# Two orders on TensorE in layer AB: values' second half ahead of q and k in the first loop; the time step's projection behind the first product with v

## The chip, the cores and the metric

The kernel is one program on one core of a Trainium2 chip. Time is the device time of one execution in microseconds (us); the profile's times are counted from the start of its span. The engines are TensorE (PE: matmuls and transposes, its weight loads listed apart as PEld), VectorE (DVE), ScalarE (ACT), GpSimd (POOL), and SyncE (SP), whose queue issues nearly all DMAs.

## What is computed

One inference step of a two-layer streaming encoder, for a prompt of 2048 tokens and a sample of 32 tokens that share all weights. The first layer (AB in the kernel) normalizes x and projects it with one input matrix. Group A is a gated linear attention with 4 heads of 64 keys and 128 values:

```
q_a, k_a, v_a, glow, z_a, q_b, k_b, v_b, z_b = split(rms_norm(x) @ w_in)
g = log_sigmoid(glow @ w_gate_up + b_gate) / 16              # decay per token and key
per chunk:  b = cumsum(g);  qe = q * exp(b)
   o = tril(qe @ (k * exp(-b)).T) @ v + qe @ S
   S = exp(b_last) * S + (k * exp(b_last - b)).T @ v
o_a = rms_norm(o) * silu(z_a)
```

Group B is attention over a window of 128 rows with 8 query heads, 2 key heads, learned sinks and a position bias; its output is gated by silu(z_b). Both go through one output projection and are added to x. The second layer (C) is a Mamba-2 scan with a causal convolution; its step `dt` is a 32-column projection of the normalized output of layer AB, made by softplus, together with the running sum of dt*A over the tokens.

Outputs are y for prompt and sample, and the new states and caches.

## The kernel before

Rows of x are cut into 17 tiles: tile 0 is the sample (32 rows), tiles 1 to 16 are 128 rows each of the prompt. The program runs in phases with a barrier between them: `setup`, `layer_gla` (group A of the first layer, to about 545 us), `layer_swa` (group B, the output projection, the norm of the result and the step of layer C, to about 1355 us), `layer_c` and `project_c`. The change touches the PE programs of `layer_gla` and `layer_swa` alone.

Nothing plans the order of work. Each engine has its own program, written out by hand, and runs it strictly in order; semaphores join them. `tiles(start, step, end, eng)` calls `start` for tile 0, `step(x, n, m)` for each tile x with its two successors n and m, and `end` for the last one. `since(eng, sem, x, back, n)` waits until `sem` has been raised by the tile `back` ahead of x. Almost every product is made three times (high part by high part, high by low, low by high), so a projection with KT = 8 slices of 128 rows has 24 matmuls.

**layer_gla.** In `step(x, n, m)` PE projects tile n, finishes the attention of tile x and turns (transposes) tile m. The order is: `queries_keys(n)` (512 columns into bank B_QK), `attention(x)` (key by query products, L732, and the turned decayed keys, L737), `values(n)`, `gate_low(n)` (L751), `outputs(x)` (L774, L775, L779), `turn_qk(n)`, `gate_up(n)`, `turn_x(m)`, `gate(n)` (z, 512 columns into B_ZA), `turn_oa(x)` (L792). `values(n)` projects the second half of the values with the low-rank gate (272 columns, bank B_VG, L708), then the first half (256 columns, L744) and group B's k and v (256 columns, L708), both into B_V0. All projections but L744 are made by the helper `project`, so they share L708 and are told apart by their columns.

The psum has eight banks and some serve twice. B_ZA and B_QK are one bank: q and k of tile n may be written once DVE has made z's gate of tile x (`za_made`, L622). B_H, into which x is turned, is B_V0 and B_VG: both may be written again once DVE has taken the low part of the turned tile (`h_low`). On SP, `load_x` of the next tile stands behind the two stores of the gated output of the tile before (`store_oa`).

In `start`, tile 0 is projected while the weights still arrive: each slice k of the first projection waits for its weights (`w_low`, L565), the later projections find them made.

**layer_swa.** In `step(x, n, m)` PE's order is: `scores(x)`, `queries(n)`, `turn_weights(x, 0)` (L1415), `turn_x1(before)` (L1462), `gate(n)`, `steps_in(before)` (L1472, the projection for the time step), `turn_weights(x, 1)`, `weighted(x, 0)` (L1425, L1426: product of the softmax weights of heads 0 to 3 with v), `time_step(before)` (L1480, turns of dt and its running sum), `output_start(x, 0)` (12 matmuls of 512 columns, L1434), `weighted(x, 1)`, `output_start(x, 1)`, `turn_ob(x)`, `turn_q(n)`, `turn_k(n)`, `output_end(x)`. `before` is the tile ahead of x; the first step has none.

What feeds these: `steps_in(before)` needs the turned x1 of `before` in SBUF (`h2_half`, DVE L1250). `weighted(x, half)` needs the turned weights of that half copied to SBUF, one part by ACT (`pt0_copied`, L1039) and one by DVE (`pt1_copied`, L1208). ACT's order there is `weights_turned(x, 0)`, `time_step(before)` (L1066 to L1069: abs, exp, ln; needs `steps_in`), `window_gate(n)` (a table load L1084, tanh L1087, a table load L1088), `weights_turned(x, 1)`. DVE's order is `weights_turned(x, 0)`, `window_in(n)`, `turned_x1(before)`, `time_step(before)` (four small instructions, the last a scan, `dtac_made`), `weights_turned(x, 1)`, `weighted(x, 0)` (L1216), `time_step_tok(before)` (L1269, `dtok_made`), `window_gate(n)`, `weighted(x, 1)`.

The two halves of the output projection have a bank each, B_OUT[0] and B_OUT[1]. The turned x1 uses both, and the time step's projection and turns use the second (B_DT and B_DTT). Therefore the first half waited for both, turned x1 taken and token form copied:

```python
if n == 0:
    pe.wait_ge(s["oa_in"], 32 * x.t + 32)
    since(pe, s["dtok_made"], x, 1)
    since(pe, s["h2_half"], x, 1, 2)
```

Of the kernel before, what the change touches and what calls it, by code (L numbers as in the profile page):

```python
# [45 lines left out]
A_V1, A_KV = VA + 256, QB  # L46
A_VG = 256 + RANK
# [9 lines left out]
def names(nc, phase, text):  # L57

    return {n: nc.alloc_semaphore(f"{phase}_{n}") for n in text.split()}
# [227 lines left out]
def since(eng, sem, x, back, n=1):  # L287

    if not x.fixed or x.t >= back:
        eng.wait_ge(sem, n * (x.t - back + 1))  # L290


def layer_gla(nc, a, o, c, d, w, psum):

    with ExitStack() as ctx:
        def sb(name, shape, dtype=F32):
# [27 lines left out]
        s = names(nc, "gla", """w_high w_low x_in s0_in hT_out0 hT_out1 kv_out0 kv_out1 oa_out s_out  # L324
            act_x act_g act_o dve_x dve_g dve_o init0
            ssq_x var_x rs_x rstd_x xn_made h_full h_high h_low
            qk_full qk_copied vg_full v0_full vg_copied v0_copied glt_full glow_copied qkt_full
            gup_full g_abs g_ln b_scal eb_made q_made s_scaled kd_full kd_copied att_full att_copied
            za_full za_tanh za_made o_full o_sq o_var o_ln oa_made sup_full s_new oat_full oat_high oat_low""")
        block = ctx.enter_context(nc.Block())  # L330
        xp = a["x_prompt"][0].rearrange("(t r) m -> t r m", r=P)
        B_O, B_OAT, B_QK, B_V0, B_VG, B_G, B_ATT, B_QKT = psum
# [366 lines left out]
        def _(pe):  # L699
            M, T = nc.tensor.matmul, nc.tensor.transpose  # L700

            def project(out, x, col, n, full):

                for k in range(KT):
                    if x.sample:
                        pe.wait_ge(s["w_low"], k + 1)
                    for p, (h, wt) in enumerate(((hh, wh), (hh, wl), (hl, wh))):
                        ins = M(out, h[x.buf][:, k, 0:x.R], wt[:, k, col:col + n],  # L708
                                start=(k == 0 and p == 0), stop=(k == KT - 1 and p == 2))
                ins.then_inc(full, 1)  # L710

            def turn_x(x):
                pe.wait_ge(s["xn_made"], x.t + 1)
                since(pe, s["vg_copied"], x, 1)
                since(pe, s["v0_copied"], x, 1)
                for k in range(KT):
                    ins = T(B_H[k // 4][:, (k % 4) * P:(k % 4) * P + x.R], xn[0:x.R, k * P:(k + 1) * P], c["ident"][0:x.R, 0:x.R])
                    if k % 4 == 3:
                        ins.then_inc(s["h_full"], 1)

            def queries_keys(x):
                pe.wait_ge(s["h_low"], 2 * x.t + 2)
                since(pe, s["za_made"], x, 1)
                project(B_QK[0:x.R, :], x, 0, 512, s["qk_full"])

            def attention(x):
# [10 lines left out]
                    ins = T(B_KD[0:R, j * P:(j + 1) * P], ekd[:, j, 0:R], c["ident"][:, :])  # L737
                ins.then_inc(s["kd_full"], 1)

            def values(x):  # L740
                project(B_VG[0:x.R, 0:A_VG], x, A_V1, A_VG, s["vg_full"])
                for k in range(KT):
                    for p, (h, wt) in enumerate(((hh, wh), (hh, wl), (hl, wh))):
                        M(B_V0[0:x.R, 0:256], h[x.buf][:, k, 0:x.R], wt[:, k, VA:VA + 256],  # L744
                          start=(k == 0 and p == 0), stop=(k == KT - 1 and p == 2))
                project(B_V0[0:x.R, 256:512], x, A_KV, 256, s["v0_full"])

            def gate_low(x):
                pe.wait_ge(s["vg_copied"], x.t + 1)
                since(pe, s["b_scal"], x, 1)  # L750
                T(B_G[0:RANK, 0:x.R], vg[x.buf][0:x.R, 512 + 256:512 + A_VG], c["ident"][0:x.R, 0:x.R]).then_inc(s["glt_full"], 1)  # L751
# [31 lines left out]
            def gate(x):  # L783
                pe.wait_ge(s["qk_copied"], x.t + 1)
                project(B_ZA[0:x.R, :], x, ZA, 512, s["za_full"])
# [9 lines left out]
            def start(x, n):  # L795
                pe.wait_ge(s["init0"], 3)
                turn_x(x)
                queries_keys(x)
                values(x)
                gate_low(x)  # L800
                turn_qk(x)
                gate_up(x)
                turn_x(n)
                gate(x)

            def step(x, n, m):
                queries_keys(n)
                attention(x)
                values(n)
                gate_low(n)  # L810
                outputs(x)
                turn_qk(n)
                gate_up(n)
                if m is not None:
                    turn_x(m)
                gate(n)
                turn_oa(x)

            def end(x):
                attention(x)  # L820
                outputs(x)
                turn_oa(x)

            tiles(start, step, end, pe)
    return s


def layer_swa(nc, a, o, c, d, w, psum):

    with ExitStack() as ctx:  # L830
        def sb(name, shape, dtype=F32):
# [29 lines left out]
        s = names(nc, "swa", """w_in0 w_in1 w_high w_low kcache_in h_in kv_in oa_in x1_in fin_out x1_out hT_out dt_out  # L861
            act_q act_p act_n act_dt dve_q dve_k dve_m dve_d dve_n dve_dt
            init0 kcache_full kcache_kept pool_step kv_shifted bias_set
            qb_full qb_sq q_summed kv_sq v_copied qb_var qb_ln qn_made kn_made qtr_full qT_made ktr_full kz_made
            zb_full zb_tanh zb_made sc_full sc_added mx_made p_made pt_full pt0_copied pt1_copied pv_full pv_taken
            otr_b ob_high ob_low out_full x1_made x1_sq x1_var x1_ln x1_rstd xn2_made h2_full h2_half
            dt_full dt_abs dt_ln dtac_made dttr_full dtok_made""")
# [508 lines left out]
        def _(pe):  # L1376
            M, T = nc.tensor.matmul, nc.tensor.transpose

            def project(out, x, col, full):

                for k in range(KT):
                    if x.sample:
                        pe.wait_ge(s["w_low"], k + 1)
                    for p, (h, wt) in enumerate(((hh, wh), (hh, wl), (hl, wh))):
                        ins = M(out, h[:, k, 0:x.R], wt[:, k, col:col + 512],  # L1385
                                start=(k == 0 and p == 0), stop=(k == KT - 1 and p == 2))
                ins.then_inc(full, 1)
# [30 lines left out]
            def weighted(x, half):  # L1418
                R = x.R
                pe.wait_ge(s["pt0_copied"], 2 * x.t + half + 1)  # L1420
                pe.wait_ge(s["pt1_copied"], 2 * x.t + half + 1)
                pe.wait_ge(s["v_copied"], x.t + 1)
                for h in range(4):
                    out = B_PV[half][0:R, h * P:(h + 1) * P]
                    M(out, pT[:, 0, h, 0:R], vprev[:, :], start=True, stop=False)  # L1425
                    ins = M(out, pT[0:R, 1, h, 0:R], vcur[0:R, :], start=False, stop=True)  # L1426
                ins.then_inc(s["pv_full"], 1)
# [10 lines left out]
            def output_start(x, n):  # L1438
                if n == 0:
                    pe.wait_ge(s["oa_in"], 32 * x.t + 32)  # L1440
                    since(pe, s["dtok_made"], x, 1)
                    since(pe, s["h2_half"], x, 1, 2)
                partial(x, n, 0)

            def turn_ob(x):
# [20 lines left out]
            def steps_in(x):  # L1466
                t, R = x.t, x.R
                pe.wait_ge(s["h2_half"], 2 * t + 2)
                if x.sample:
                    pe.wait_ge(s["kcache_in"], 64)  # L1470
                for k in range(KT):
                    ins = M(B_DT[0:HC, 0:R], wdt[:, k, :], h1T[:, k, 0:R], start=(k == 0), stop=(k == KT - 1))  # L1472
                ins.then_inc(s["dt_full"], 1)

            def time_step(x):
                R = x.R
                pe.wait_ge(s["init0"], 3)
                pe.wait_ge(s["dtac_made"], x.t + 1)
                for e in range(2):
                    ins = T(B_DTT[0:R, P + e * HC:P + (e + 1) * HC], dtac[:, e, 0:R], c["ident"][0:HC, 0:HC])  # L1480
                ins.then_inc(s["dttr_full"], 1)
# [25 lines left out]
            def step(x, n, m):  # L1507
                first = x.fixed and x.t == 0
                before = None if first else Tile(x.t - 1, 1 - x.buf)
                scores(x)  # L1510
                queries(n)
                turn_weights(x, 0)
                if before is not None:
                    turn_x1(before)
                gate(n)
                if before is not None:
                    steps_in(before)
                turn_weights(x, 1)
                weighted(x, 0)
                if before is not None:  # L1520
                    time_step(before)
                output_start(x, 0)
                weighted(x, 1)
                output_start(x, 1)
                turn_ob(x)
                turn_q(n)
                turn_k(n)
                output_end(x)
# [807 lines left out]
```

## Time and profile before

| | us |
|---|---|
| three runs | 3242.59, 3244.75, 3246.57; median 3244.75 |
| profiled execution | 3245.2, span 3243.4 |
| PE busy | 2931.4 (90% of the span) |
| PE weight loads busy | 2485.5 (77%) |
| DVE busy | 1876.6 (58%) |
| ACT busy | 1412.8 (44%) |
| DMA | 280.87 MB, mean 87 GB/s |
| mean granted TensorE clock | 0.968 |

In the rows further down, a timeline row gives start, duration, engine, line, operation, output<-inputs, the types' shapes and a count; neighbours that are alike are merged into one row. In brackets stands the time that the engine was idle ahead of it and what released it. A matmul's duration is longer than the distance to the next one, since they are pipelined; the distance between starts is what a group costs. "issue" as a releaser means that the profile shows nothing that the engine waited for. The granted clock (PEclk) is 1.00 for full speed, 2.4 GHz, and 0.50 for 1.2 GHz.

### The profile page before, as it was taken

Reading aid. Unit: us, or ns where it says so; the run is one execution under the profiler, and the core shown is the slowest. Engines: PE = TensorE matmul, PEld = TensorE weight load, DVE = VectorE, ACT = ScalarE, POOL = GpSimd, SP = SyncE. Lnnn points to the kernel's source line nnn. Section 1 sums busy time; section 2 is a strip of 40 time slices with the busy share of each in tenths; the row PEclk is TensorE's granted clock in tenths of the full one; section 3 lists DMA queues with packets and bytes.
Section 4 is the critical chain, followed back from the end, with each engine's and each line's share of the span. In section 5 each row is a group of like instructions: output and inputs, shape, how many; then the busy total and the mean of one; then the engine's idle time right before and its main releaser. Section 6 shows DMA issues by size and latency. Waiting matters only on the chain. (4 is left out here: it accounts for less than half of the span.)

```text
span 3243.4 us, 50025 instructions
## 1 busy us (share of the span) xinstructions
PE 2931.4 (90%) x18074; PEld 2485.5 (77%) x18074; DVE 1876.6 (58%) x4799; ACT 1412.8 (44%) x2901; POOL 61.3 (2%) x166
## 2 busy tenths in 40 slices
PE   4999996688888888599999999999999999879999
PEld 2788886266666666489997999889997999758787
DVE  3343343344443444268887888878887888842322
ACT  2455553333333333245555555545555555521211
POOL 0000000000000000000000000000000000000000
PEclk9999998699999999799999999999999999989999
DMA  4122212322212221332213221142123211144443
GB/s 144 71 83 82 82 71 71 122 73 82 82 65 75 79 80 59 127 114 65 64 60 102 83 64 59 51 133 65 59 62 100 66 61 60 53 170 137 131 145 111
DMA packets 148699, 280.87 MB, mean 87 GB/s; under 512 B 46359, under 2 KB 69402, under 8 KB 144378
## 3 DMA queue, kind: packets, MB, share of 16 engines
q1 hardware_dynamic: 147042, 276.55, 26.0%
q10 hardware_dynamic: 1560, 3.05, 0.3%
q8 instruction: 58, 0.95, 0.1%
q14 instruction: 39, 0.32, 0.0%
HBM read 204.29 MB, written 75.26 MB: 86 GB/s over the span
## 5 line engine op out<-in xcount | busy, mean ns | idle before, releaser
L2060 PEld LDWEIGHTS bank<-hT_c,w_group 128*128 128x128 f32 x6528 | 749.5, 192 | 39.1 <-issue 33.5
L2060 PE MATMUL bank<-hT_c,w_group 128*128 128x128 f32 x6528 | 750.9, 275 | 0.0
L1884 DVE SCALAR_TENSOR_TENSOR conv_acc<-u,convw,conv_acc 128x128 f32<-128x128 f32 (+1 forms) x1224 | 331.4, 339 | 10.4 <-ACT conv_acc L1818 8.0
L2047 PE MATMUL bank<-wz_high,h_high 128*128 128x512 f32 (+1 forms) x544 | 239.2, 440 | 13.5 <-DVE wz_low L1965 13.5
L708 PE MATMUL bank<-wa_high,hT_high 128*128 128x512 f32 (+5 forms) x544 | 191.0, 351 | 43.2 <-DVE za L622 26.0
L2285 PE MATMUL bank<-wout_high,yT_high 128*128 128x512 f32 (+1 forms) x544 | 212.6, 391 | 6.4 <-DVE wout_low L2254 6.4
L2047 PE MATMUL bank<-wz_low,h_high 128*128 128x512 f32 (+1 forms) x544 | 215.3, 396 | 0.0
L2047 PE MATMUL bank<-wz_high,h_low 128*128 128x512 f32 (+1 forms) x544 | 214.9, 395 | 0.0
L2285 PE MATMUL bank<-wout_low,yT_high 128*128 128x512 f32 (+1 forms) x544 | 212.5, 391 | 0.0
L2285 PE MATMUL bank<-wout_high,yT_low 128*128 128x512 f32 (+1 forms) x544 | 212.5, 391 | 0.0
L708 PE MATMUL bank<-wa_low,hT_high 128*128 128x512 f32 (+5 forms) x544 | 187.2, 344 | 0.0
L708 PE MATMUL bank<-wa_high,hT_low 128*128 128x512 f32 (+5 forms) x544 | 187.1, 344 | 0.0
L2218 ACT ACTIVATE yT_high<-yT_in 128x2048 fp32r<-128x2048 f32 (+1 forms) x34 | 62.6, 1841 | 275.1 <-PE bank L2285 260.8
L1772 ACT ACTIVATE u<-bank 128x256 f32<-128x256 f32 (+1 forms) x68 | 25.5, 376 | 323.0 <-PE bank L2060 323.0
L1818 ACT ACTIVATE conv_acc<-u,vec,convw 128x128 f32<-128x128 f32 (+1 forms) x408 | 162.4, 476 | 7.0 <-ACT u L1772 3.0
L2262 DVE TENSOR_TENSOR x_in<-x_in,bank 128x512 f32<-128x512 f32 (+1 forms) x34 | 23.4, 687 | 220.6 <-PE bank L2285 220.6
L708 PEld LDWEIGHTS bank<-wa_high,hT_high 128*128 128x128 f32 (+1 forms) x544 | 100.3, 184 | 64.5 <-issue 34.1
L1434 PE MATMUL bank<-wout_high_ab,oT_high 128*128 128x512 f32 (+1 forms) x272 | 110.6, 407 | 38.6 <-DVE oT_low L1221 20.6
L1385 PE MATMUL bank<-wb_high,h0T_high 128*128 128x512 f32 (+1 forms) x272 | 117.2, 431 | 29.7 <-DMA h0T_low<-h0T_low_d 20.4
L2047 PEld LDWEIGHTS bank<-wz_high,h_high 128*128 128x128 f32 (+1 forms) x544 | 101.7, 187 | 51.8 <-issue 30.6
L2103 PE MATMUL bank<-xdt,ed 128*128 128x128 f32 (+1 forms) x1088 | 132.7, 275 | 3.1 <-DVE ed L1941 3.1
L2103 PEld LDWEIGHTS bank<-xdt,ed 128*128 128x128 f32 (+1 forms) x1088 | 125.9, 187 | 5.6 <-DVE ed L1941 5.3
(289 smaller groups left out, 5812.1 us busy)
## 6 DMA issues: line engine op xcount, KB each, us to landing
hT_c<-h1T SPq DMA_DIRECT2D x64, 512.0 KB, 3.3
acb<-acT SPq DMA_DIRECT2D x64, 512.0 KB, 3.7
yT_in<-yT SPq DMA_DIRECT2D x32, 1024.0 KB, 5.2
yT<-yT_t SPq DMA_DIRECT2D x64, 256.0 KB, 3.1
xin<-in_x_prompt SPq DMA_DIRECT2D x16, 512.0 KB, 3.7
h0T_high_d<-hT_high SPq DMA_DIRECT2D x16, 512.0 KB, 2.6
h0T_low_d<-hT_low SPq DMA_DIRECT2D x16, 512.0 KB, 3.4
h0T_high<-h0T_high_d SPq DMA_DIRECT2D x16, 512.0 KB, 3.4
```

The source lines that it names most:

```text
L708: ins = M(out, h[x.buf][:, k, 0:x.R], wt[:, k, col:col + n], start=(k == 0 and p == 0), stop=(k == KT - 1 and p == 2))
L1385: ins = M(out, h[:, k, 0:x.R], wt[:, k, col:col + 512], start=(k == 0 and p == 0), stop=(k == KT - 1 and p == 2))
L1434: ins = M(B_OUT[n][0:x.R, :], y[:, k, 0:x.R], wt[:, k, 512 * n:512 * n + 512], start=(k == 0 and p == 0), stop=(k == KT - 1 and p == 2))
L1772: A(ub[:, 4:6, 3:3 + R], B_BC[:, 0:2 * P].rearrange("p (j r) -> p j r", j=2)[:, :, 0:R], ACT.Copy).then_inc(s["u1_made"], 1)
L1818: ins = A(acc[:, i, 0:R], ub[:, i, 3:3 + R], ACT.Identity, scale=c["convw"][:, 3 * CT + ct:3 * CT + ct + 1], bias=c["vec"][:, V_CB + ct:V_ ...
L1884: ins = V.scalar_tensor_tensor(acc[:, i, 0:R], ub[:, i, tap:tap + R], c["convw"][:, tap * CT + ct:tap * CT + ct + 1], acc[:, i, 0:R], ALU. ...
L2047: ins = M(B_Z[0:x.R, :], h[:, k, 0:x.R], wt[:, k, :], start=(k == 0 and p == 0), stop=(k == KT - 1 and p == 2))
L2060: ins = M(out, wg[x.g % 2][:, k, j * P:(j + 1) * P], hT[x.buf][:, k, :], start=(k == 0), stop=(k == KT - 1))
L2103: ins = M(B_INTRA[h // 4][0:R, (h % 4) * P:(h % 4 + 1) * P], ed[0:R, h, 0:R], xdt[0:R, (h // 2) * P:(h // 2 + 1) * P], start=True, stop=True)
L2218: nc.scalar.activation(yh[x.buf][:, :, 0:x.R], yT[x.buf][:, :, 0:x.R], ACT.Copy).then_inc(s["y_high"], 1)
L2262: V.tensor_tensor(x[0:R, :], x[0:R, :], psum[cur.buf][0:R, :], ALU.add).then_inc(s["sum_made"], 1)
L2285: ins = nc.tensor.matmul(psum[i][0:R, :], y[:, k, 0:R], wt[:, k, :], start=(k == 0 and p == 0), stop=(k == K - 1 and p == 2))
```

## The change

In `layer_gla`, the projection of values' second half leaves `values` and becomes `values_gate`, which stands ahead of `queries_keys` in `start` and in `step`. The wait for `h_low` moves with it; the wait for `za_made` stays at q and k.

In `layer_swa`, inside `step`, `steps_in(before)` moves from behind `gate(n)` to behind `weighted(x, 0)`, and `time_step(before)` from there to behind `weighted(x, 1)`. In `output_start` each half now waits for what used its own bank: the first for the turned x1, the second for the token form of the time step. `end` keeps its order, and uses the changed `output_start`.

```diff
             def queries_keys(x):
-                pe.wait_ge(s["h_low"], 2 * x.t + 2)
                 since(pe, s["za_made"], x, 1)
                 project(B_QK[0:x.R, :], x, 0, 512, s["qk_full"])
...
+            def values_gate(x):
+                pe.wait_ge(s["h_low"], 2 * x.t + 2)
+                project(B_VG[0:x.R, 0:A_VG], x, A_V1, A_VG, s["vg_full"])
+
             def values(x):
-                project(B_VG[0:x.R, 0:A_VG], x, A_V1, A_VG, s["vg_full"])
...
             def start(x, n):
                 pe.wait_ge(s["init0"], 3)
                 turn_x(x)
+                values_gate(x)
                 queries_keys(x)
                 values(x)
...
             def step(x, n, m):
+                values_gate(n)
                 queries_keys(n)
                 attention(x)
                 values(n)
...
             def output_start(x, n):
                 if n == 0:
                     pe.wait_ge(s["oa_in"], 32 * x.t + 32)
+                    since(pe, s["h2_half"], x, 1, 2)
+                else:
                     since(pe, s["dtok_made"], x, 1)
-                    since(pe, s["h2_half"], x, 1, 2)
                 partial(x, n, 0)
...
                 gate(n)
-                if before is not None:
-                    steps_in(before)
                 turn_weights(x, 1)
                 weighted(x, 0)
                 if before is not None:
-                    time_step(before)
+                    steps_in(before)
                 output_start(x, 0)
                 weighted(x, 1)
+                if before is not None:
+                    time_step(before)
                 output_start(x, 1)
```

## Rows read from the trace of the kernel before

**Rows 1.** The page, busy time of PE, with its share of the span.

```profile
PE 2931.4 (90%) x18074; PEld 2485.5 (77%) x18074; DVE 1876.6 (58%) x4799; ACT 1412.8 (44%) x2901; POOL 61.3 (2%) x166
```

**Rows 2.** Waits: who waited for whom: us in total, times, longest.

```profile
PE bank L708 <- DVE za L622: 26.0, 16, 1.7
...
PE bank L1472 <- DVE h1T_t L1250: 50.8, 17, 3.4
```

**Rows 3.** Timeline, PE, one tile of layer_gla.

```profile
341.14 0.60 PE L792 MATMUL bank<-ident,za 128*128 128x128 f32 x4
343.38 0.47 PE L708 MATMUL bank<-wa_high,hT_high 128*128 128x512 f32 x1 [1.64 <-DVE za L622]
...
349.03 1.05 PE L732 MATMUL bank<-qz,ek 128*128 128x128 f32 x8
...
350.06 0.37 PE L708 MATMUL bank<-wa_high,hT_high 128*128 128x272 f32 x1
...
353.16 0.28 PE L744 MATMUL bank<-wa_high,hT_high 128*128 128x256 f32 x1
...
358.92 0.39 PE L774 MATMUL bank<-v_tok,attm 128*128 128x128 f32 x2
```

**Rows 4.** Timeline, DVE and ACT, the same tile.

```profile
342.55 0.68 DVE L622 SCALAR_TENSOR_TENSOR za<-za,bank 128x512 f32<-128x512 f32 x1
...
352.21 0.75 DVE L628 COPY_PREDICATED attm<-causal,bank 128x512 f32<-128x512 uint32 x1
...
349.91 1.06 ACT L421 ACTIVATE xn<-xin 128x1024 f32<-128x1024 f32 x1 [5.97 <-DMA xin<-in_x_prompt]
```

**Rows 5.** Timeline, PE, the sample's tile at the start of layer_gla.

```profile
68.77 0.64 PE L708 MATMUL bank<-wa_high,hT_high 128*32 128x512 f32 x1 [2.60 <-DVE wa_low L565]
...
70.06 0.43 PE L708 MATMUL bank<-wa_high,hT_high 128*32 128x272 f32 x1
...
73.68 0.32 PE L708 MATMUL bank<-wa_low,hT_high 128*32 128x272 f32 x1
...
74.71 0.28 PE L744 MATMUL bank<-wa_high,hT_high 128*32 128x256 f32 x1
```

**Rows 6.** Timeline, PE, one tile of layer_swa.

```profile
932.36 1.94 PE L1472 MATMUL bank<-h1T_t,wdt 128*32 128x128 f32 x16 [3.02 <-DVE h1T_t L1250]
934.23 1.09 PE L1415 MATMUL bank<-ident,sc 128*128 128x128 f32 x8
...
937.04 0.31 PE L1480 MATMUL bank<-ident,dtac 32*128 32x32 f32 x2
938.47 0.47 PE L1434 MATMUL bank<-wout_high_ab,oT_high 128*128 128x512 f32 x1 [1.12 <-issue]
...
941.32 0.38 PE L1425 MATMUL bank<-vprev,pT 128*128 128x128 f32 x2
...
943.02 0.48 PE L1434 MATMUL bank<-wout_high_ab,oT_high 128*128 128x512 f32 x1
```

**Rows 7.** Timeline, ACT, the same tile.

```profile
934.33 0.36 ACT L1066 ACTIVATE dtw<-bank,dtb 32x128 f32<-32x128 f32 x1 [4.77 <-PE bank L1472]
...
937.30 1.28 ACT L1088 ACT_TABLE_LOAD   x1
938.60 0.60 ACT L1039 ACTIVATE pT<-bank 128x512 f32<-128x512 f32 x1
```

**Rows 8.** Timeline, DVE, the same tile.

```profile
938.15 0.21 DVE L1269 COPY dtok_t<-bank 128x64 f32<-128x64 f32 x1
```

**Rows 9.** Windows (us, busy and count by engine, PEclk, DMA) and timeline, PE, two other tiles.

```profile
716.00:718.00 2.00, 2.00 (x10) 1.67 (x11) 0.00 (x0) 0.00 (x0) 0.00 (x0) 0.50 1.02 418
...
715.90 3.36 PE L1472 MATMUL bank<-h1T_t,wdt 128*32 128x128 f32 x16 [3.02 <-DVE h1T_t L1250]
...
723.43 0.47 PE L1434 MATMUL bank<-wout_high_ab,oT_high 128*128 128x512 f32 x1 [1.12 <-issue]
...
1274.60 3.05 PE L1472 MATMUL bank<-h1T_t,wdt 128*32 128x128 f32 x16 [3.10 <-DVE h1T_t L1250]
```

## The prediction

> **What bounds the kernel now.** I read the shares of busy time first: TensorE (PE) is busy 90% of the span [rows 1], and it is the only engine whose idle time can be worth tens of microseconds. Then the waits, for PE alone: two of the longest stand at places that the change touches [rows 2]. In layer A, q and k wait 26.0 us in 16 goes for z's gate (it frees the bank that q and k share with z). In layer B, the time step's projection waits 50.8 us in 17 goes for the turned x1. Then the timeline of one tile of each loop, engine by engine, to see what stands around each wait; it shows a third one, 1.12 us behind the time step's turns in every tile of layer B [rows 6].
>
> **Layer A, the wait at q and k.** Before: the turns of the gated output start at 341.14, q and k at 343.38 after 1.64 us of idle [rows 3]; z's gate on DVE runs 342.55 to 343.23 and frees them [rows 4]. After: values' second half (24 products of 272 columns) needs h_low only, which `queries_keys` also waited for, so it starts when the turns are through, near 341.7. It lasts 3.10 us (350.06 to 353.16 [rows 3]) and ends near 344.8, 1.5 us after the gate is made. So the wait goes whole, 26.0 us over 16 tiles; the matmuls are the same in number and form, so nothing else changes on PE.
>
> What is late next? The attention products now stand behind values' second half: they end 3.1 - 1.7 = 1.4 us later than now, near 351.5. What waits for them is DVE's mask (352.21 to 352.96, behind the norm of the next x) and ACT's copy of the turned keys behind the same norm [rows 4]. The norm begins when its x has landed (ACT is idle 5.97 us for that DMA) and does not hang on PE; so both stay where they are. The outputs, which need the mask, come 5.76 us behind the attention products (353.16 to 358.92 [rows 3]), near 357.2: 4.2 us of cover are left of 5.9. SP's queue keeps its order: each load of x stands behind the two stores of oa, which hang on z's gate, and keeps its distance from the gate. I take 0 for all of this; its bounds are 0 and 1.64 us per tile (then a second wait has taken the first one's place whole).
>
> **Layer A, the start.** With the sample's tile PE follows the weights as they are made: the last trio of q and k starts at 68.77, each 0.43 us apart, and values' second half at 70.06 [rows 5]. After, the paced trios are those of 272 columns, 0.23 us each (sixteen in the 3.62 us from 70.06 to 73.68), and 24 products of 512 columns follow instead of 24 of 272. Until 73.68 the products take twice the time that they take from there on [rows 5], so: last trio 68.77 to 69.45; ten products at 0.43 us to 73.7; fourteen at 0.23 us (the pitch of q and k in rows 3: 24 in 5.65 us) to 77.0; there values' first half starts, against 74.71 now. Cost 2.3 us; if the clock rose only after all of q and k it would be 4.2. Layer A: -26.0 + 2.3 = **-23.7 us**.
>
> **Layer B, order alone.** I count from S, the start of the time step's projection (932.36 in rows 6). Now: projection S to S+1.87, then turned weights of half 1 and the first product with v (2.81 us) to S+4.68, the time step's turns, 1.12 us of idle (until DVE, busy with the copy of half 1 and the gating, has copied the token form, 938.15 to 938.36 [rows 8]), first output projection S+6.11 to S+8.96, second product with v to S+10.66, and there the second output projection starts [rows 6]. Ahead of S PE is idle 3.02 us.
>
> After: turned weights and the first product with v (2.81 us) fill the idle time ahead of S. S itself stays, since DVE's turned x1 sets it and nothing ahead of that moved; 0.2 to 0.5 us of the wait are left. Then: projection to S+1.87, first output projection (2.85 us) to S+4.72. The second product with v needs ACT's copy of half 1, and that stands behind the time step's logs, two table loads and the tanh of the window gate: ACT's first instruction of this chain starts 1.97 us after S and the copy ends 938.60 + 0.60, S+6.84 [rows 7]. This chain hangs on the projection alone, so it stays; the first output projection that covered it came later till now. So a **new wait of 2.0 us** (the last matmul runs on to about S+4.9; next start S+6.9). DVE's copy of half 1 comes behind the scan, which is done before the turns at S+4.68, and is no later than ACT's. Second product with v: 1.70 us, to S+8.6. Turns 0.31, DVE's copy 0.21 and some 0.1 of handing over, with nothing ahead of it on DVE: S+9.3, where the second output projection starts. Against S+10.66: **-1.3 us**. What follows (turned output, q, k, the wait for oT_low) is told off from there and keeps its length; SP's store of the token form and POOL's copies come no later than what they serve. On 15 tiles: -19.5. The last tile, outside the loop, keeps its order, but its first output projection no longer waits for the token form: -1.1.
>
> **Layer B, clock.** In 9 of the 15 tiles the granted clock is at 0.50 (1.2 GHz, where 1.00 is 2.4) for some 3.4 us from around S on, as in the slice 716 to 718, and at full speed before and after [rows 9]. Those tiles take 7.5 to 7.7 us from S to the first output projection (715.90 to 723.43 in the first of the nine; the last has its S at 1274.60 [rows 9]) instead of 6.11 [rows 6]; 1.42 us more in that one and 1.61 in each of the others, 14.3 us in all. Each time PE had been idle 3.0 to 3.3 us just before. Idle spells of 1.64 us in layer A and of 1.12 us in layer B are never followed by it. After the change the spell ahead of S is at most 0.5 us, so these nine go: **-14.3**. The new 2.0 us spell lies between the two groups, nearer to 1.64; I take one such stretch in 15 tiles, +1.6, with 0 and 15 (+24) as bounds.
>
> The Trainium skill, page "TensorE: Matmul & The Clock Gate", section on why this matters for your kernels, says that idle gaps between bursts of matmuls put the clock back to half rate, and so speaks for the first half of this and against the new spell. Its summary would count the old spells of 3.0 to 3.3 us as just harmful; that six of 15 were not shows that the spell's length alone doesn't decide.
>
> **Sum.** -23.7 - 19.5 - 1.1 - 14.3 + 1.6 = -57.0 us. The profiled execution took 3245.2 us (span 3243.4 and 1.8 around it), 0.5 above the median of the three runs. 3245.2 - 57.0 = **3188 us**. The two layers behind, two thirds of the span, are untouched and start earlier by the same amount; their own few stretches at half clock (ahead of each weight change) may fall otherwise, some 3 us either way.
>
> **Rivals.**
> - *The new spell costs the clock.* Place: the second product with v, 15 tiles, 1.6 us each. For it: 2.0 us is longer than any spell that was harmless in rows 3 and 6, besides those six of 3.0 us and more. Five tiles: 3188 + 6.5 = 3195; all: 3188 + 22.4 = 3210. Chance 0.22.
> - *The wait in layer A comes back elsewhere* (the mask, or ACT's copies of the values behind a late x): nothing gained there, the start's 2.3 us paid: 3188 + 26 = 3214. Against it: 4.2 us of cover for the mask. If only half comes back: 3201. Chance 0.08.
> - *The old stretches at half clock stay*, because the remains of the wait and the new spell do what the long spell did: 3188 + 12.7 = 3201. Chance 0.05.
> - *Slower: ACT holds the second product with v.* The copy of half 1 is the last of ACT's chain with two table loads. Were each load to hold ACT for as long again as its own row (1.28 us, at 937.30 [rows 7]), the copy would end at S+9.4, the spell would be 4.5 us and end in half clock each time: 2.6 + 1.6 = 4.2 us on 15 tiles is 63, less the one stretch already counted: 3188 + 61 = 3249. It decides from 3.8 us per tile on. Against it: ACT's copy starts at 938.60, 0.02 us behind the load's end. Chance 0.03. The Trainium skill, page "ScalarE: Activation LUTs", section "What ACT_TABLE_LOAD costs", gives 1283 ns for the load and some 1380 ns of drain on top for each switch; the load's length agrees with the row to the digit, the drain is not to be seen behind it, and by the page the estimate would be this rival's.
> - *It does nothing*, as the waits belong to something else than the named releasers: 3245. Chance 0.01.
>
> **How the numbers follow.** The forecast, with none to three new stretches and 3 us of play behind, is 3181 to 3194, chance 0.61. The range down to 3181 and up to 3207 takes in most of the clock rivals and half a return in layer A, and leaves some 0.2 outside. A measurement of this kernel tells 0.2% (6.5 us) from no change. All cases but the last two are faster by more: faster 0.95, same 0.02, slower 0.03.
>
> **What would show it.** PE's wait for z's gate at q and k: gone, and no new one at the attention products or the outputs. The tile of layer A: shorter by 1.64 us. The wait ahead of the time step's projection: 0.2 to 0.5 us instead of 3.0. A wait of 2.0 us at the second product with v, released by ACT's copy of the turned weights, and 0.5 us or so ahead of the second output projection. Granted clock 1.00 through layer B's loop. I'm wrong if that clock shows 0.50 there in more than three tiles, if the mask on DVE becomes late, or if the start costs more than 5 us.

## The result, and the profile after

The changed kernel takes 3186.4 us (median of 4 runs, 3183.4 to 3193.2) against 3243.7 of the kernel before beside it: ratio 0.9828, 95% interval 0.9807 to 0.9849. That is 57 us less by the medians, and 49 to 63 us by the interval. Repeated later it gave 3187.3 us, ratio 0.9824 (0.9808 to 0.9840). The profiled execution is the slowest of the four: 3193.2 us, span 3191.4.

The page after, to be read against [rows 1]: PE's busy time is nearly what it was, the span is shorter, so PE's share is 92% where it was 90%.

```profile
PE 2926.8 (92%) x18074; PEld 2483.7 (78%) x18074; DVE 1873.8 (59%) x4799; ACT 1413.4 (44%) x2901; POOL 61.4 (2%) x166
```

The waits of PE in layer B after the change (us in total, times, longest). Against [rows 2]: PE waits for z's gate at q and k no more, the wait for the turned x1 fell from 50.8 to 11.0 us, and a new one of 29.6 us in 15 goes stands at the second product with v, released by ACT's copy.

```profile
PE bank L1429 <- ACT pT L1043: 29.6, 15, 2.0
...
PE bank L1477 <- DVE h1T_t L1254: 11.0, 16, 2.9
...
PE bank L1438 <- DVE dtok_t L1273: 4.7, 15, 0.3
```

One tile of layer A on PE (timeline; compare [rows 3]). Both groups of 24 projections (values' second half, then q and k) now stand between the turns and the attention products, and PE has no idle time among them. From one start of the outputs to the next it is 26.19 us (341.29 to 367.48).

```profile
325.39 0.60 PE L794 MATMUL bank<-ident,za 128*128 128x128 f32 x4
325.75 0.37 PE L708 MATMUL bank<-wa_high,hT_high 128*128 128x272 f32 x1
...
334.44 1.05 PE L731 MATMUL bank<-qz,ek 128*128 128x128 f32 x8
...
335.46 0.36 PE L746 MATMUL bank<-wa_high,hT_high 128*128 128x256 f32 x1
...
341.29 0.39 PE L776 MATMUL bank<-v_tok,attm 128*128 128x128 f32 x2
...
367.48 0.39 PE L776 MATMUL bank<-v_tok,attm 128*128 128x128 f32 x2
```

The same tile on DVE and ACT ([rows 4]): z's gate is made at 327.5, long before q and k are due, and the mask at 337.1, 4.2 us before the outputs.

```profile
326.81 0.68 DVE L622 SCALAR_TENSOR_TENSOR za<-za,bank 128x512 f32<-128x512 f32 x1
336.38 0.74 DVE L628 COPY_PREDICATED attm<-causal,bank 128x512 f32<-128x512 uint32 x1
...
334.07 1.06 ACT L421 ACTIVATE xn<-xin 128x1024 f32<-128x1024 f32 x1 [5.88 <-DMA xin<-in_x_prompt]
```

One tile of layer B on PE at full clock ([rows 6]). From the start of the time step's projection (S, 773.80) the second output projection is 9.49 us off; before it was 10.66.

```profile
773.80 1.93 PE L1477 MATMUL bank<-h1T_t,wdt 128*32 128x128 f32 x16 [0.68 <-DVE h1T_t L1254]
...
775.67 0.50 PE L1438 MATMUL bank<-wout_high_ab,oT_high 128*128 128x512 f32 x1
...
780.69 0.49 PE L1429 MATMUL bank<-vprev,pT 128*128 128x128 f32 x2 [1.96 <-ACT pT L1043]
...
782.67 0.31 PE L1485 MATMUL bank<-ident,dtac 32*128 32x32 f32 x2
783.29 0.50 PE L1438 MATMUL bank<-wout_high_ab,oT_high 128*128 128x512 f32 x1 [0.32 <-DVE dtok_t L1273]
```

ACT in the same tile ([rows 7]): the chain from the projection to the copy is as long as before, S+1.98 to S+6.84.

```profile
775.78 0.36 ACT L1070 ACTIVATE dtw<-bank,dtb 32x128 f32<-32x128 f32 x1 [4.75 <-PE bank L1477]
...
778.74 1.28 ACT L1092 ACT_TABLE_LOAD   x1
780.04 0.60 ACT L1043 ACTIVATE pT<-bank 128x512 f32<-128x512 f32 x1
```

In what follows a spell is idle time of PE, and a stretch is the time that the granted clock then stays at 0.50. In two of the 15 tiles of the loop (S at 686.0 and 729.8) the clock fell right after the new spell of 2.0 us, and each stretch was 6.8 us long, twice as long as each of the nine before ([rows 9]). Windows: length, busy and count of PE, PEld, DVE, ACT, POOL, then PEclk, DMA share, GB/s.

```profile
692.00:694.00 2.00, 1.08 (x8) 1.08 (x9) 0.00 (x0) 0.85 (x2) 0.00 (x0) 0.93 0.00 0
694.00:696.00 2.00, 2.00 (x11) 1.77 (x10) 0.00 (x0) 0.00 (x0) 0.00 (x0) 0.50 0.00 0
696.00:698.00 2.00, 1.69 (x6) 1.36 (x6) 1.15 (x3) 0.00 (x0) 0.29 (x1) 0.50 0.08 16
698.00:700.00 2.00, 2.00 (x6) 1.52 (x6) 0.00 (x0) 0.00 (x0) 0.00 (x0) 0.50 0.00 0
```

Where the time went in the two profiled executions, by the start of the first PE instruction of each phase: layer B's phase begins 29.1 us earlier (567.3, now 538.2; 1.5 of it because the last weights came earlier in this execution), layer C's 56.3 earlier (1359.0, now 1302.7), the last phase 51.7 earlier (2859.9, now 2808.2). So layer A gave 29.1 (27.6 without the weights), layer B 27.2, and layer C, whose code is the same, took 4.6 back: the clock was at 0.50 there for 64.9 us, and for 54.6 before. The profiled execution gained 52 us in all. A second one, further down, was an execution of 3187.1 us; there layer A gave 29.7, layer B 33.0, and layer C took 5.0 back.

### The profile page after: what moved, and what is told of

The parts are those of the page before. It is cut to its first block and busy times, and to the rows that moved or that the text cites. A ratio compares the mean times of both kernels' runs of the same rounds, so it can differ in the third digit from the quotient of the medians.

```text
span 3191.4 us, 50009 instructions
## 1 busy us (share of the span) xinstructions
PE 2926.8 (92%) x18074; PEld 2483.7 (78%) x18074; DVE 1873.8 (59%) x4799; ACT 1413.4 (44%) x2901; POOL 61.4 (2%) x166
## 5 line engine op out<-in xcount | busy, mean ns | idle before, releaser
L1389 PE MATMUL bank<-wb_high,h0T_high 128*128 128x512 f32 (+1 forms) x272 | 117.2, 431 | 29.7 <-DMA h0T_low<-h0T_low_d 19.6
L2052 PEld LDWEIGHTS bank<-wz_low,h_high 128*128 128x128 f32 (+1 forms) x544 | 102.0, 188 | 35.5 <-issue 14.4
```

Of the source, the lines that this page charges most:

```text
L1389: ins = M(out, h[:, k, 0:x.R], wt[:, k, col:col + 512], start=(k == 0 and p == 0), stop=(k == KT - 1 and p == 2))
L2052: ins = M(B_Z[0:x.R, :], h[:, k, 0:x.R], wt[:, k, :], start=(k == 0 and p == 0), stop=(k == KT - 1 and p == 2))
```

## The experiments

The times are medians; each ratio is against runs of the kernel before on the same chip.

**Layer A alone, and layer B alone.** The edits are the halves of the diff.

> Only the edit in layer A (values' second half ahead of q and k); layer B as before. My theory by the profile after: the 16 boundaries give 1.9 us each (a tile took 28.10 and takes 26.19), the start costs 2.4, so 28 us less than before: about 3216. The forecast's own term was 23.7: 3220. Rival (the gain in layer A was lent by layer B, which starts otherwise): less than 20.

> Only the edits in layer B. Theory: 15 tiles by 1.17 us of order = 17.5, nine old stretches at half clock gone = 14.3, 1.1 at the end, less 2.85 for each new stretch (0 to 5 of them): 19 to 33 us less than before, about 3216. The new wait for ACT's copy of half 1 shows as 15 times 2.0 us. Rival (clock not affected by the order): 18 to 19 less and the stretches at half clock stay near nine.

Measured: layer A alone 3217.4 us, ratio 0.9925 (0.9908 to 0.9942), some 24 us by the ratio and 28 by the medians; layer B alone 3212.0 us, ratio 0.9899 (0.9886 to 0.9912), 33 us. The product of the two ratios is 0.9825, and the whole change has 0.9828: within the intervals the two gains add. Layer A's six runs are spread over 19.5 us (3208.9 to 3228.4), and its interval, 19 to 30 us, doesn't quite shut out the rival (less than 20). The trace does: layer A's tile takes 26.19 us there as well, and layer B, from its first S to its last, takes 666.3 us against 669.6, so it gives nothing back. For layer B the rival falls: there is one stretch at half clock in the loop of the profiled execution, where it asked for about nine. Layer A alone keeps eight such stretches in layer B, which starts some 34 us earlier (533.6 against 567.3): an earlier start of the layer doesn't remove them. PE's waits of layer B alone:

```profile
PE bank L1425 <- ACT pT L1039: 29.6, 15, 2.0
...
PE bank L1473 <- DVE h1T_t L1250: 10.4, 15, 2.9
```

**The long idle spell left in place.** In layer B's step, shown against the changed kernel:

```diff
                 gate(n)
+                if before is not None:
+                    steps_in(before)
                 turn_weights(x, 1)
                 weighted(x, 0)
-                if before is not None:
-                    steps_in(before)
                 output_start(x, 0)
                 weighted(x, 1)
```

> Layer B with the time step's projection left behind the gate as before, and only the time step's turns moved behind the second product with v and the bank waits split. The long idle spell ahead of the projection (3.0 to 3.4 us) stays, the 1.12 us behind the turns go, and no new wait of 2.0 us comes, since the first product with v and the output projection cover ACT again. Layer A as in the changed kernel. Theory (the long spell makes the half clock): about nine stretches at 0.50 stay in the loop; order alone gives 0.55 us on 15 tiles, so with layer A's 28 about 3208. Rival (the sum of the idle time in a tile, 4.3 us, makes it): the stretches go or fall to half, about 3200.

The kernel that ran had layer A as before, not as that text says, so layer A's 28 us belong on both its numbers: theory 3236, rival 3228. Measured: 3237.2 us, ratio 0.9983 (0.9973 to 0.9993), 5.5 us less than before by the ratio. The wait of 1.12 us behind the turns is gone (0.3 us are left of it), the spell ahead of the projection is there, and no wait for ACT's copy appears. The clock decides between theory and rival: 13 of the 15 tiles have a stretch at 0.50. So the rival falls, as there is less idle time per tile than before and there are more stretches, not fewer. The theory's "about nine" was too few. Timeline and windows of one such tile: the clock falls some 0.5 us ahead of the projection (0.90 in the slice up to 840.00, in which PE does nothing), within the idle spell of 3.08 us.

```profile
840.07 3.34 PE L1473 MATMUL bank<-h1T_t,wdt 128*32 128x128 f32 x16 [3.08 <-DVE h1T_t L1250]
...
851.32 0.50 PE L1434 MATMUL bank<-wout_high_ab,oT_high 128*128 128x512 f32 x1 [0.32 <-DVE dtok_t L1269]
```

```profile
838.00:840.00 2.00, 0.00 (x0) 0.00 (x0) 1.97 (x6) 0.00 (x0) 0.00 (x0) 0.90 0.91 326
840.00:842.00 2.00, 1.93 (x10) 1.60 (x11) 0.02 (x1) 0.00 (x0) 0.00 (x0) 0.50 1.00 408
842.00:844.00 2.00, 2.00 (x14) 1.65 (x13) 0.16 (x1) 0.52 (x2) 0.00 (x0) 0.75 0.13 53
```

**The changed kernel again.**

> The changed kernel itself, once more, for its spread and for the number of stretches at half clock in layer B's loop. Theory: the new spell of 2.0 us lies at the edge, so the number differs between executions, 0 to 5 of 15, 2.85 us each, and with it the time, 3181 to 3194. Rival (always the same two tiles): two stretches again, around 692 and 736.

Measured: 3187.3 us, five runs from 3181.7 to 3194.0. In its profiled execution the loop of layer B has no stretch at half clock, against two in the first; the kernel with the old start, below, has the same loop and had two, each 3.4 us long. So the number of stretches differs between executions, as the theory said.

**ACT's copy ahead of the window gate.** In ACT's step:

```diff
                     time_step(before)
-                window_gate(n)
                 weights_turned(x, 1)
+                window_gate(n)
                 ob_high(x)
```

> The changed kernel with ACT's copy of half 1 ahead of the window gate's table load, tanh and table load. Theory (the new 2.0 us wait is those 3.2 us and nothing else): the copy ends 3.7 us after the start of the time step's projection, before the output projection's first half is through at 4.7, so the wait goes whole: 1.9 to 2.0 us on 15 tiles, and no new stretch at half clock: 28 to 36 us less than the changed kernel, about 3155. Rival (DVE's copy behind its scan, or the window gate that comes later, takes its place): a wait of 1 us or more remains at the second product with v or appears at the turned output.

Measured: 3151.2 us, ratio 0.9717 (0.9704 to 0.9729): 35 us less than the changed kernel. The wait for the copy is gone from PE's waits and no other took its place; the second output projection comes at S+7.50 (9.49 before the edit), and no tile of the loop sees half clock. 15 x 1.99 = 29.8 us are the order. The rest fits the stretches that the changed kernel has in some executions and a layer C that is shorter by 6.2 us (1499.3 against 1505.5), with the clock at 0.50 there for 47.8 us and not 64.9; why the clock falls less in layer C isn't known. PE and ACT in one tile:

```profile
759.92 1.94 PE L1477 MATMUL bank<-h1T_t,wdt 128*32 128x128 f32 x16 [0.68 <-DVE h1T_t L1254]
...
767.42 0.50 PE L1438 MATMUL bank<-wout_high_ab,oT_high 128*128 128x512 f32 x1 [0.32 <-DVE dtok_t L1273]
```

```profile
762.84 0.57 ACT L1043 ACTIVATE pT<-bank 128x512 f32<-128x512 f32 x1
763.43 1.28 ACT L1088 ACT_TABLE_LOAD   x1
```

**Two more table loads in the window gate.**

```diff
                 act.preload_act_table_set("exp_and_others")
+                act.preload_act_table_set("natural_log_exp_and_others")
+                act.preload_act_table_set("exp_and_others")
```

> The changed kernel with two more table loads in the window gate of each tile (ACT only, same results). The new wait ahead of the second product with v becomes 2.0 + 2 x 1.28 = 4.5 us. Theory (ACT's chain sets that product, and a long spell brings half clock): 2.57 us on 16 tiles = 40, and half clock behind nearly each spell, 1.6 to 2.85 us on 13 more tiles = 21 to 37: 3247 to 3263. Rival (the clock needs more than the spell): 3226.

Measured: 3268.5 us, ratio 1.0070 (1.0056 to 1.0084): 0.7% slower than the kernel before, as in the forecast's fourth rival, and 5 us beyond the expected range. The wait is 4.58 us, as worked out, so each added load costs its own 1.28 us and nothing behind it:

```profile
742.56 1.28 ACT L1088 ACT_TABLE_LOAD   x1
743.85 1.28 ACT L1089 ACT_TABLE_LOAD   x1
745.14 1.28 ACT L1090 ACT_TABLE_LOAD   x1
746.43 0.60 ACT L1093 ACTIVATE zb<-bank 128x512 f32<-128x512 f32 x1
```

The excess is the clock: all 15 tiles have a stretch at 0.50. In 11 of them it is 10.2 us long, three times those of before; in the other four it is 3.4. A tile with a long one took 47.4 us from S to S (692.17 to 739.53), where a tile of the changed kernel at full clock took 40.9: 2.57 of it are the loads, 3.9 the clock. Timeline and windows of the next tile:

```profile
748.99 0.80 PE L1431 MATMUL bank<-vprev,pT 128*128 128x128 f32 x2 [4.58 <-ACT pT L1043]
753.43 0.80 PE L1440 MATMUL bank<-wout_high_ab,oT_high 128*128 128x512 f32 x1 [0.32 <-DVE dtok_t L1275]
```

```profile
748.00:750.00 2.00, 1.01 (x4) 1.01 (x5) 0.00 (x0) 0.93 (x2) 0.00 (x0) 0.59 0.00 0
...
756.00:758.00 2.00, 2.00 (x6) 1.52 (x6) 0.00 (x0) 0.00 (x0) 0.00 (x0) 0.50 0.00 0
```

**The old order in layer A's start.**

```diff
                 turn_x(x)
-                values_gate(x)
+                pe.wait_ge(s["h_low"], 2 * x.t + 2)
                 queries_keys(x)
+                values_gate(x)
                 values(x)
```

> The changed kernel with the old order in start alone (q and k paced by the weights, then values' second half). Theory: 2.4 us less than the changed kernel, seen in the start of values' first half against the last weights: 5.9 us behind instead of 8.3. Rival: nothing, as the first tile's later work waits for x.

Measured: 3184.1 us, ratio 0.9810 (0.9798 to 0.9823); the changed kernel has 0.9824 and 0.9828, and the intervals overlap, so the time alone doesn't show it. The trace shows the start: values' first half starts 5.47 us behind the last trio's start (66.68 to 72.15), in the changed kernel 8.31 (67.28 to 75.59), in the kernel before 5.94 [rows 5].

```profile
67.28 0.43 PE L708 MATMUL bank<-wa_high,hT_high 128*32 128x272 f32 x1 [2.35 <-DVE wa_low L565]
75.59 0.28 PE L746 MATMUL bank<-wa_high,hT_high 128*32 128x256 f32 x1
```

```profile
66.68 0.63 PE L708 MATMUL bank<-wa_high,hT_high 128*32 128x512 f32 x1 [1.93 <-DVE wa_low L565]
...
72.15 0.28 PE L746 MATMUL bank<-wa_high,hT_high 128*32 128x256 f32 x1
```

But this profiled execution gives the 2.8 us back within layer A. In the first tile of its loop the granted clock fell at 104.8 for 6.8 us, and from the sample's outputs to the next ones it took 30.6 us (100.83 to 131.41), where the changed kernel took 27.5 (104.27 to 131.74) at full clock. PE had not been idle ahead of this fall; it came right behind the sample's small products (32 rows).

```profile
102.00:104.00 2.00, 2.00 (x12) 1.01 (x11) 0.00 (x0) 0.36 (x3) 0.00 (x0) 1.00 0.19 66
104.00:106.00 2.00, 2.00 (x9) 1.31 (x9) 1.30 (x4) 1.07 (x6) 0.00 (x0) 0.69 0.00 0
106.00:108.00 2.00, 2.00 (x11) 1.77 (x10) 0.84 (x4) 1.23 (x4) 0.00 (x0) 0.50 0.00 0
```

**No cover for the attention products.**

```diff
                 queries_keys(n)
-                attention(x)
                 values(n)
+                attention(x)
                 gate_low(n)
```

> The changed kernel with layer A's attention products behind all of the values, straight ahead of the low gate's turn and the outputs: the cover for DVE's mask and ACT's copies, 5.8 us, goes to none. Theory (4.2 us of cover were left): waits of some 1.0 to 1.5 us appear per tile, on the mask or on the copy of values that stands behind the copy of the turned keys on ACT: 16 to 24 us more than the changed kernel, about 3206. Rival (something else covers them): same as the changed kernel.

Measured: 3203.4 us, ratio 0.9878 (0.9864 to 0.9893), 17 us more than the changed kernel. The wait shows at the low gate's turn, and not on the mask. It is for ACT's copy of values' second half, which stands on ACT behind the copy of the turned keys:

```profile
PE bank L753 <- ACT v_tok L446: 12.2, 16, 0.8
```

A tile takes 27.32 us instead of 26.19. So no cover at all costs 1.1 us per tile, and the late attention products of the change itself, behind which no wait appears, have cost nothing.

**Both together** (the copy ahead of the window gate, and the old order in the start).

> The changed kernel with both: ACT's copy of half 1 ahead of the window gate, and the old order in layer A's start. Theory (the two gains lie in different layers and add): 35 and 2.4 us less than the changed kernel, about 3149, with no stretch at half clock inside layer B's loop. Rival (the start's gain is swallowed by the wait for x at the first tiles): 3151.

Measured: 3152.3 us, ratio 0.9711 (0.9698 to 0.9724), the same as with the copy alone (0.9717, 0.9704 to 0.9729). Both are faster than the changed kernel by some 35 us and than the kernel before by 93; whether the start's edit still gives its 2.4 us there is not shown. The arrival of the weights moved by more between these executions (last trio at 69.58 here), and both had the fall of the clock in layer A's first tile, 3.4 us long with the copy alone and 6.8 with both.

## Why the prediction was right

It said 3188, and 57.0 us less; measured 3186.4 and 57 less. The mechanisms are those forecast, and an experiment or a trace stands behind each. That the sum agrees to the microsecond is luck: layer A gave 4.0 us more than forecast, and layer B's order gave 2.0 less. Layer C took some 5 us that stood at 0 in the sum, and the new stretches cost 6.0 us in one profiled execution and nothing in the other, where 1.6 stood. The two executions gained 52 and 58 us.

- *Layer A's loop.* Forecast 26.0, found 30.0: 1.90 us at 14 boundaries (a tile of 28.08 to 28.10 us before, as from 330.82 to 358.92 by the starts of the outputs, now 26.19) and 1.69 at the two with the sample's tile. The mechanism was right. The step that was mis-sized is "it starts when the turns are through, near 341.7": the idle time of a row counts from the modelled end of the last matmul, but the next group starts inside that matmul's tail, 0.36 us behind the turns' start (325.39 to 325.75) and not 0.60. The wait's price was 1.9 us where its row says 1.64. The attention products came 1.2 us later behind the turns and the mask kept 4.2 us of cover, as worked out; with no cover at all the price was 1.1 us per tile, not 1.64.
- *Layer A's start.* Forecast 2.3, found 2.4 (8.31 less 5.94). The trace of the kernel with the old start has 2.8 less than the changed kernel; its time can't resolve it.
- *Layer B, order.* Forecast 1.3 us per tile with a new wait of 2.0; found 1.17 and 2.0, 17.5 us over the loop instead of 19.5. Of the old wait ahead of the projection 0.4 to 0.7 us are left, where 0.2 to 0.5 were forecast. The new wait is right in place, releaser and length, and the copy's reorder shows that nothing else hid behind it. The part that was short is the end: the product and turns until the second output projection took 2.60 us (780.69 to 783.29) and not 2.4. In the last tile, outside the loop, the 1.12 us ahead of the first output projection are gone as well (16 such waits before, none now); the 1.1 us forecast for it can't be told off in time, as the clock differs there.
- *Layer B, clock.* The nine stretches went, 14.3 us, as forecast; with the long spell left in place there were 13. Of the new stretches one was forecast, by a choice and not by a mechanism, at 1.6 us, the price of a stretch of 3.4 us. In the first profiled execution there were two, 6.8 us long, and they cost 3.0 us each (S to S 43.8 and 44.0 us against 40.9). In four other profiled executions with this loop there were none, one, two and two, of 3.4 us each, at 1.5 us or so (S to S 42.4).
- *The layers behind.* Unchanged code, 4.6 us longer in the profiled execution, more than the 3 us of play that the forecast gave. The clock was at 0.50 there for 64.9 us against 54.6, in the second profiled execution too. Over all eleven profiled executions layer C takes 1499 to 1502 us with 47.8 to 58.0 us at half clock, 1503 with 61.4 and 1505.5 to 1505.9 with 64.9. What places these stretches wasn't tried.
- *The slower rival.* Its premise is false: a load holds ACT for 1.28 us and nothing more. What it drew from the premise is right: with the copy made late by two more loads, a spell of 4.6 us ends in half clock each time and the kernel is slower than before.

The Trainium skill, page "ScalarE: Activation LUTs", section "What ACT_TABLE_LOAD costs", adds a drain of some 1380 ns to each switch. No run shows it: three loads in a row start 1.29 us apart and the tanh follows 0.01 us behind the third.

## What to carry to other kernels

When work that needs nothing is moved into an idle spell, look at which other engine's chain hung on the work that was moved the other way: here ACT's two table loads and a tanh stood between the time step and a copy that PE needed, and moving one line on ACT gave 35 us, where the whole change had given 57. Price a wait by the distance between starts around it, not by its idle time alone. And count an idle spell of PE twice: once for itself, and once for the matmuls behind it if the granted clock falls.

## What the runs showed of the hardware

- Idle spells of PE ahead of the projection, 2.5 to 3.4 us long, come with a stretch at half clock in 9 of 15 tiles (kernel before), 8 (layer A alone) and 13 (projection left in place). One of layer A alone's eight came with a spell of 2.5 us, and the longest spell of the kernel before, 3.44 us, had none. Spells of 2.0 us ahead of the second product with v are followed by one in 2, 0, 1, 2 and 2 of 15 tiles in the five profiled executions that have them; spells of 4.6 us in 15 of 15; spells of 1.1 and 1.6 us never. So there is no sharp length; what else decides wasn't separated.
- An idle spell isn't needed. In the first tile of layer A's loop the clock fell for 3.4 to 6.8 us, at 104.8 to 107.6, in four of the eleven profiled executions. In three of them (old start, copy ahead, both) PE had had no idle time over 0.4 us for more than 20 us ahead; the clock fell during the sample's small products (32 rows) or within 1.1 us of their end, and they stood in the same place in the executions without a fall. A stretch of 3.4 us cost 1.6 us there and one of 6.8 us 3.1 (29.07 and 30.59 us from outputs to outputs against 27.47).
- The length of a stretch varies at one and the same place. At the projection, with dense products behind it, it was 3.4 us in 29 of 30 cases and 6.8 in one. At the second product with v, where two short waits follow (0.3 and 1.2 us), it was 3.4 us in five cases and 6.8 in two; with the added loads it was 10.2 us in 11 tiles and 3.4 in four. That the short waits make it longer is not shown, as the same work stood behind the short ones.
